# A third pair of steps by seven block products in each gated network, and the input sums one step earlier

## The reference

```python
def swiglu(x, w_gate, w_up, w_down):
    return (jax.nn.silu(x @ w_gate) * (x @ w_up)) @ w_down

        f = swiglu(rms_norm_2(x, g[0]), ffn_w_gate[layer, 0], ffn_w_up[layer, 0], ffn_w_down[layer, 0])
        x = x + 0.5 * rms_norm_2(f, g[1])
        ...
        f = swiglu(rms_norm_2(x, g[4]), ffn_w_gate[layer, 1], ffn_w_up[layer, 1], ffn_w_down[layer, 1])
```

## Time and profile before

| | |
|---|---|
| median of 3 runs | 1821.15 us (1819.73 to 1822.6) |
| profiled execution, its own time | 1819.23 us |
| its span in the profile | 1817.4 us |
| PE busy | 1761.6 us, 97% of the span, 10314 matmuls and as many weight loads |
| DVE busy | 1390.4 us, 77% |
| ACT busy | 996.4 us, 55% |
| share of PE in the chain that ended last | 82% |
| share of DVE in it | 13% |

### The profile page before, as it was taken

The page is one execution under the profiler, slowest core; times in us unless marked ns, Lnnn a source line. Parts: engine busy times, 40 slices in busy tenths (PEclk is TensorE's granted clock), DMA queues, the critical chain, the costliest instruction groups (busy, mean ns, idle before and its releaser), DMA issues.

```text
span 1817.4 us, 25221 instructions
## 1 busy us (share of the span) xinstructions
PE 1761.6 (97%) x10314; PEld 1486.6 (82%) x10314; DVE 1390.4 (77%) x1646; ACT 996.4 (55%) x1206; POOL 58.2 (3%) x98
## 2 busy tenths in 40 slices
PE   9999999999999999899999998999999999998998
PEld 8998898888887887787898987878777878787877
DVE  5349876889888898878498778776787667878784
ACT  5446653577777676545442455545555455664453
POOL 0040000000000001000000000000000010010000
PEclk9999999999999999999999999999999999999999
DMA  9343344699899896264342034527343745143632
GB/s 378 118 171 130 117 159 163 247 356 351 334 357 350 340 374 248 96 255 189 136 165 99 18 124 155 232 107 307 143 167 134 301 158 185 52 164 117 275 140 80
DMA packets 51380, 363.02 MB, mean 200 GB/s; under 512 B 5697, under 2 KB 5825, under 8 KB 8642
## 3 DMA queue, kind: packets, MB, share of 16 engines
q1 hardware_dynamic: 50976, 359.24, 51.8%
q10 hardware_dynamic: 290, 2.17, 0.3%
HBM read 360.34 MB, written 1.05 MB: 199 GB/s over the span
## 4 chain that ended last, share of the span: by engine, by line
PE 82%; DVE 13%; ACT 3%; issue 1%; DMA 1%; POOL 0%; DVEq 0%; POOLq 0%; ACTq 0%
PE bank L2858 8%; PE bank L3441 4%; PE bank L3416 4%; PE bank L3418 4%; PE bank L3417 4%; PE bank L3442 4%; PE bank L3443 4%; PE bank L3270 3%; PE bank L3272 3%; PE bank L3271 3%; PE bank L3475 3%; PE bank L3476 3%; PE bank L3477 3%; PE bank L2916 2%; DVE w_a L1716 2%; PE bank L3287 2%
## 5 line engine op out<-in xcount | busy, mean ns | idle before, releaser
L1716 DVE TENSOR_TENSOR w_a<-ring,w_a 128x2048 fp32r<-128x2048 f32 x220 | 500.6, 2288 | 157.3 <-ACT w_a L995 156.4
L995 ACT ACTIVATE w_a<-ring 128x2048 fp32r<-128x2048 f32 x219 | 416.3, 1912 | 118.6 <-PE bank L3443 50.6
L1716 DVE TENSOR_TENSOR w_b<-ring,w_b 128x2048 fp32r<-128x2048 f32 x63 | 144.1, 2287 | 37.2 <-ACT w_b L995 37.1
L995 ACT ACTIVATE w_b<-ring 128x2048 fp32r<-128x2048 f32 x63 | 120.5, 1913 | 35.8 <-DMA ring<-in_stream 14.8
L2858 PE MATMUL bank<-h,w_a 128*128 128x256 f32 x1040 | 137.3, 285 | 1.0 <-DVE ring_lo L1821 1.0
L2858 PEld LDWEIGHTS bank<-h,w_a 128*128 128x128 f32 x1040 | 128.8, 191 | 4.1 <-issue 3.0
L3441 PE MATMUL bank<-w_a,hid 128*128 128x512 f32 x280 | 112.8, 403 | 19.1 <-DVE hid L2341 19.1
L3442 PE MATMUL bank<-w_a,hid 128*128 128x512 f32 x280 | 111.0, 397 | 0.0
L3443 PE MATMUL bank<-w_a,hid 128*128 128x512 f32 x280 | 110.8, 396 | 0.0
L3416 PE MATMUL bank<-w_a,h 128*128 128x512 f32 x240 | 94.9, 396 | 0.5 <-DVE w_a L1716 0.5
L3418 PE MATMUL bank<-w_a,h 128*128 128x512 f32 x240 | 93.7, 390 | 0.0
(11 more groups left out here) (648 smaller groups left out, 4215.6 us busy)
## 6 DMA issues: line engine op xcount, KB each, us to landing
ring<-in_stream SPq DMA_DIRECT2D x330, 1024.0 KB, 5.4
G<-in_gains SPq DMA_DIRECT2D x14, 512.0 KB, 7.6
cmp_area<-in_cmp_w ACTq DMA_DIRECT2D x1, 2048.0 KB, 11.3
sm<-in_small SPq DMA_DIRECT2D x1, 1582.0 KB, 12.0
con<-in_consts SPq DMA_DIRECT2D x1, 1032.0 KB, 16.0
X<-in_x SPq DMA_DIRECT2D x2, 512.0 KB, 4.1
out_x<-X SPq DMA_DIRECT2D x4, 256.0 KB, 2.0
sm<-in_small SPq DMA_DIRECT2D x1, 730.5 KB, 22.7
```

The source lines that it names most:

```text
L995: act.activation(w_slot(unit)[:, 0, :], ring[:, unit % RING, :], ACT.Copy).then_inc(S("w_hi"), 1)
L1716: dve.tensor_tensor(w_slot(unit)[:, 1, :], ring[:, unit % RING, :], w_slot(unit)[:, 0, :].bitcast(FP32), ALU.subtract).then_inc(S("w_lo"), 1)
```

## The change

Three pairs in place of two, at steps 2, 5 and 8, with one single step (1, 4, 7) before each and step 10 behind the last. The sums are made elsewhere in the order: `x_raw` in step 0 ahead of `hid_made(0, 1)`, `s1` to `s4` behind it, `x_left` still ahead of step 1. The sums of a pair's weights now all stand in the one single step before it: t1 and t3 behind `hid_left`, t2, t4 and t2_lo behind `hid_made(s, 1)`. On ACT `xs_hi` is made ahead of the high half of unit 5, and the rounding of t2 behind the silu of the second tile.

```diff
-PAIRS = (3, 7)
+PAIRS = (2, 5, 8)
...
+                def x_sums_high():
+                    act.wait_ge(S("ffn_dve"), ffn_at(FFN_DVE, name, "s4"))
+                    act.activation(xs_hi[:, :, :, :], x_sum, ACT.Copy).then_inc(S("ffn_act"), 1)
+
...
                 silu(0, 1)
+                x_sums_high()
                 split_at(5)
...
                     hid_in(s - 1, range(0, 2))
+                    split_at(3 * s + 3)
+                    silu(s, 1)
                     if s + 1 in PAIRS:
                         pair_ahead(PAIRS.index(s + 1), s + 1)
-                    split_at(3 * s + 3)
-                    silu(s, 1)
                     split_at(3 * s + 4)
                     split_at(3 * s + 5)
...
                 split_at(4)
+                x_whole()
                 hid_made(0, 1)
+                x_sums()
                 split_at(5)
+                x_left()
                 for s in range(1, last):
...
+                    ahead = PAIRS.index(s + 1) if s + 1 in PAIRS else None
                     hid_made(s, 0)
                     hid_left(s - 1, range(0, 2))
-                    if s + 1 == PAIRS[0]:
-                        x_left()
+                    if ahead is not None:
+                        weight_sums(ahead, s + 1)
                     split_at(3 * s + 3)
-                    if s + 1 in PAIRS:
-                        last_weight_sum(PAIRS.index(s + 1), s + 1)
                     hid_made(s, 1)
-                    if s + 1 in PAIRS:
-                        ring_left(f"t2_hi_{PAIRS.index(s + 1)}", pair_units(name, s + 1)[0])
+                    if ahead is not None:
+                        more_weight_sums(ahead, s + 1)
+                        ring_left(f"t2_hi_{ahead}", pair_units(name, s + 1)[0])
                     split_at(3 * s + 4)
                     split_at(3 * s + 5)
-                    if s + 2 in PAIRS:
-                        if s + 2 == PAIRS[0]:
-                            x_sums()
-                        weight_sums(PAIRS.index(s + 2), s + 2)
```

More of the change, by code:

```diff
@@ L671, in build @@
         PAIR_DVE = ["t1", "t3", "t2", "t4", "t2_lo", "u2", "t4_lo", "u3", "c21", "t1_lo", "w", "c12", "c22"]
-        FFN_DVE = ["x_raw", "s1", "s2", "s3", "s4"] + [f"{step}_0" for step in PAIR_DVE[:3]] + ["s_lo"] + [f"{step}_0" for step in PAIR_DVE[3:]] \
-            + [f"{step}_{i}" for i in range(1, len(PAIRS)) for step in PAIR_DVE]
+        FFN_DVE = ["x_raw", "s1", "s2", "s3", "s4", "s_lo"] + [f"{step}_{i}" for i in range(len(PAIRS)) for step in PAIR_DVE]
         FFN_ACT = ["s_hi"] + [f"{step}_{i}" for i in range(len(PAIRS)) for step in ("t2_hi", "m1", "t4_hi", "t1_hi")]
@@ L1392, in silu_of @@
                     act.activation(sil[:, t, :], src[:, 0:UC], ACT.Silu, scale=rn[:, t:t + 1]).then_inc(S("silu"), 1)
+                def x_sums_high():
+                    act.wait_ge(S("ffn_dve"), ffn_at(FFN_DVE, name, "s4"))
+                    act.activation(xs_hi[:, :, :, :], x_sum, ACT.Copy).then_inc(S("ffn_act"), 1)
                 def pair_ahead(i, s):
[L1395 to L1398, removed]
+                    if i:
                         act.wait_ge(S("ffn_pe"), ffn_at(FFN_PE, name, f"m5_{i - 1}"))
@@ L2345, in own, with x_whole @@
                     dve.wait_ge(S("ffn_dve"), ffn_at(FFN_DVE, name, step))
+                def x_whole():
+                    dve.wait_ge(S("h_lo"), HI0[name] + 4)
+                    dve.tensor_tensor(x_raw, h_hi[:, :, :].bitcast(FP32), h_lo[:, :, :].bitcast(FP32), ALU.add).then_inc(S("ffn_dve"), 1)
                 def x_sums():
-                    dve.tensor_tensor(x_raw, h_hi[:, :, :].bitcast(FP32), h_lo[:, :, :].bitcast(FP32), ALU.add).then_inc(S("ffn_dve"), 1)
                     own("x_raw")
@@ L2363, in weight_sums @@
                         dve.wait_ge(S("ffn_pe"), ffn_at(FFN_PE, name, f"m5_{i - 1}"))
+                    dve.wait_ge(S(f"unit{b11 % RING}"), 16 * (b11 // RING + 1))
                     dve.wait_ge(S(f"unit{b12 % RING}"), 16 * (b12 // RING + 1))
@@ L2367, in weight_sums, with more_weight_sums @@
                     dve.tensor_tensor(raw[2], raw[3], raw[2], ALU.subtract).then_inc(S("ffn_dve"), 1)
+                def more_weight_sums(i, s):
+                    b11, b21, b12, _ = pair_units(name, s)
                     own(f"t3_{i}")
-                    dve.tensor_tensor(raw[0], raw[2], raw[0], ALU.add).then_inc(S("ffn_dve"), 1)
-                def last_weight_sum(i, s):
-                    b11, b21, _, _ = pair_units(name, s)
+                    dve.tensor_tensor(ring[:, b11 % RING, :], ring[:, b12 % RING, :], ring[:, b11 % RING, :], ALU.add).then_inc(S("ffn_dve"), 1)
                     own(f"t2_{i}")
```

## The result

The changed kernel takes 1837.03 us (median of 4 runs, 1834.06 to 1840.11), the kernel before 1820.44 in the runs beside it (1819.04 to 1822.6): ratio 1.009, 95% interval 1.007 to 1.0111. It is slower by 16.6 us. The forecast was 1832.5, 11.3 above its base, in a range of 1827.5 to 1841.

A forecast was written before the change was run, and what follows sets the result against it. PE, busy 97%, was taken as the bound, except DVE's queue just ahead of a pair. First products 47.85 us earlier, stretches behind them 59.1 longer: +11.3 on 1819.23, plus 1.9 to the median, stated as 1832.5; range 1827.5 to 1841.

The forecast's parts named there:

- The two waits in place of one (5.9, then 2.6 to 5.2): PE waits for DVE 5.9 us before `down(0)`, then 2.6 to 5.2 us before the first pair's first product of sums.
- The hole of 3.8 us on DVE: DVE stands idle 3.8 us before unit 5's low half, until ACT makes the high half put behind `xs_hi`.
- the walk: DVE's new order priced by instruction, from unit 4's low half to PE's first product of sums: 30.44 us in each network.
- The wait at the turn (1.6): PE's `turn(0)` waits about 1.6 us for `hid_made(0, 1)`, covered by the wait behind it.
- The later pairs (1.3, shown 1.0): PE waits 1.3 us for t2_lo at the second and third pair; one single step and pair take 49.4 us.
- What it costs lies inside the second wait: The slow clock behind the wait before `down(0)` adds nothing, being covered by the wait before the first product of sums.
- The clock in the second wait, taken as 0: Clock loss behind the wait before the first product of sums: bounded by 0 and 2.6 us a network, taken as 0.
- Rival A: The clock falls in the second wait too, costing 2 of the 2.6 us in each network: 1840.5; chance 0.20.
- the sum: Over four networks, 59.1 us more behind the first products of sums less 47.85 us before them: +11.3 us.
- B: Faster: ACT's high half of unit 5 does not hold DVE up, 15.2 us shorter in all: 1817; chance 0.07.
- C: No difference: later pairs' sums fit into the one single step, PE does not wait there, 10.4 us off: 1822; chance 0.05.
- D: Weights come late in the last pair, or a low half waits in a pair: up to 12 us more; chance 0.08.

The follow-up runs named there:

- Experiment 1: The changed kernel with the high half of unit 5 ahead of `xs_hi` on ACT; 1825.31 us, ratio 1.0027 to the kernel before.
- experiment 10: The changed kernel with identity matmuls on PE, 22 in the first wait and 9 in the second; 1834.87 us, ratio to before 1.0078.
- Experiments 2 and 3: The changed kernel with two pairs: in 2 at steps 2 and 6, 1840.03 us; in 3 at steps 3 and 7, as before, 1829.02 us.
- Experiment 5: The changed kernel's functions with pairs at 3 and 7, all DVE work of the sums spread into single steps; 1783.93 us, ratio 0.9791.
- experiment 4: The kernel before with only the input sums moved: `x_raw` behind `hid_left(0)`, s1 to s4 between step 1's last low halves; 1799.94 us, ratio 0.9883.

## Why the prediction was right

**The two waits in place of one (5.9, then 2.6 to 5.2): right.** Measured 5.66 to 5.67, and 2.45 to 2.79, at the low end of the span given or just under it, since `down(0)` took 7.6 to 8.0 us at the slow clock. The hole of 3.8 us on DVE was 3.78 in all four networks. From unit 4's low half to the product it was 30.46 us (1105.21 to 1135.67) where the walk had 30.44. Experiment 1 shows that the hole is ACT's order: without it the first products come 15.5 us earlier in all (the walk had 15.2), and 5.2 of that go behind the longer second waits, where the clock fell. That leaves 10.3, and the medians differ by 11.7.

**The wait at the turn (1.6): right in three networks.** 1.74, 1.53 and 1.51, and 0.65 in `ffn2`, covered by the wait behind it.

**The later pairs (1.3, shown 1.0): right.** 1.05 to 1.24 in all eight. A round in `ffn1` from the second to the third product of sums is 49.43 us (1185.26 to 1234.69), where 49.4 was forecast.

**"What it costs lies inside the second wait": shown** by experiment 10, 13.72 against 13.73 us.

**The clock in the second wait, taken as 0: this is the mis-sized term.** It fell in two networks of four. There the 24 matmuls from the first product of sums on took 7.2 us, where they took 5.6 in the other two, and the time to the second product of sums was 50.92 and 50.95 us against 49.59 and 49.62: 1.3 us each, since the next wait for t2_lo became shorter. That is 2.7 of the 3.9 us by which the stretches behind the first product exceeded the forecast. Rival A, 2 us in each network, was half true. The choice rested on the earlier trace rows, where 1.79 us of idle time left the clock alone, and on the loss of the first wait shortening the second. The shortening held (2.45 to 2.79 us); that such a wait is harmless did not.

**A term that wasn't in the sum.** Part of the light stage between `ffn0` and `ffn1` ran with the clock down, and the stage took 3.4 us more than before. The change does not touch it, and in the traces of all ten experiments, as in that of before, the clock stayed at 1.00 there. So it belongs to that execution rather than to the change; what starts it stays open. The profiled execution of the changed kernel is 0.9 us above its median and that of before 1.2 below, which is why the spans differ by 18.8 us and the medians by 16.6. Without the light stage and the second waits' clock (3.4 and 2.7) the span would have grown by 12.7, against a sum of 11.3.

**The rivals.** B (the high half of unit 5 does not hold DVE) was false in the changed kernel, and made true by hand in experiment 1 it gave 11.7 us. By my sum that would have been enough (it was to decide from 11.3 on); against the 16.6 that the change really costs it is not, and the kernel stays slower. C was false: all eight later pairs wait. D was false: PE doesn't wait in step 10.

**What the change could have had.** A third pair saves 2.4 us a network of PE's time if nothing waits. It was paid for by taking a single step away from ahead of the first pair, in which DVE's sums could have lain. Experiments 2 and 3 give the price of that step, 11.0 us. Experiment 5 shows what good use of such room is worth: with two pairs and spread sums 2.1% of the time of before. No run has three pairs without the waits, so what the third pair would then bring is not shown.

## What to carry to other kernels

When a saving on the bounding engine is fed by preparation on another, walk that engine's queue instruction by instruction up to the point where the first result is needed; here one step more ahead of it was worth 11.0 us (experiments 2 and 3), the third pair about 3.0 (experiment 2). Where two in-order queues feed each other, look for an item that waits for the other queue and stands ahead of one that the other queue wants: here two lines on ACT were worth 11.7 of 16.6 us. And price a slow clock only in stretches whose end the slowed engine itself sets: `down(1)` lost 1.5 to 2.6 us four times in the kernel before, and removing that gave 2.4 us in all.

## What the runs showed of the hardware

The granted clock fell behind idle times as short as the one that I had taken for harmless, and not every time. In experiment 1, PE in `ffn2` came out of a wait of 1.80 us at full pace and slowed within three matmuls:

```profile
1304.96 0.50 PE L3445 MATMUL bank<-w_a,hid 128*128 128x512 f32 x1 [1.80 <-DVE hid L2342]
1305.29 0.48 PE L3446 MATMUL bank<-w_a,hid 128*128 128x512 f32 x1
1305.57 0.63 PE L3447 MATMUL bank<-w_a,hid 128*128 128x512 f32 x1
```

From start to start the pace goes from 0.33 and 0.28 to 0.43 us, and it fell so behind the 1.78 us of `ffn0` as well, while in `ffn1` and `ffn3` of the same run the same wait (1.80 and 1.78 us) left it at 0.23. In experiment 4 it fell at the instruction of the earlier trace rows, behind the same 1.79 us of idle time:

```profile
1452.32 1.57 PE L2878 MATMUL bank<-con,F 128*128 128x128 f32 x8 [1.79 <-DVE F L1757]
```

It did so in experiment 5 too (behind 1.79 us at 1441.10), and not in the changed kernel (1.78 us at 1482.28). So the same idle time had both outcomes, at one and the same place in the program too. What decides between them these runs don't show.

An f32 matmul of the 128x128 identity leaves two records of 0.113 us, so 0.23 us in all, as long as one record of 512 columns in the products here (0.227 from start to start).
